# The gates' activations, the log-forget and the decays of an mLSTM block, three pieces of products later

## The chip, the cores and the metric

The kernel runs on one core of a Trainium2 chip. The metric is the device time of one execution in microseconds (us). Before the change the median of three runs is 1558.58 us (1557.95 to 1559.88).

## The reference

Two transformer blocks for 512 tokens of width 1024, in float32. The change touches the mLSTM mixer of the first block. There `proj = h @ w_in + b_in` gives, beside much else, q, k, v and two gates (input gate and forget gate) for each of four heads:

```python
log_f = jax.nn.log_sigmoid(f_pre)
b = jnp.cumsum(lfc, axis=-1)
d_log = jnp.where(causal, b[..., :, None] - b[..., None, :] + ic[..., None, :], -jnp.inf)
m_t = jnp.maximum(inter_log, jnp.max(d_log, axis=-1))
dmat = jnp.exp(d_log - m_t[..., None])
sc = jnp.einsum("bhtd,bhsd->bhts", qc, kc) * dmat
num = (jnp.einsum("bhts,bhse->bhte", sc, vc)
       + inter_w[..., None] * jnp.einsum("bhtd,bhde->bhte", qc, c_st))
```

q and k go through a causal convolution of four taps and a silu first. Another branch puts `a` through a depthwise convolution of 31 taps over 1024 channels.

## The kernel before, in words

Activations lie transposed in SBUF, 128 channels by 512 tokens for each tile. To keep float32's accuracy a product is made in three: both the weights and the activations are split into a high half (float32r) and the rest. A **product** here is one tile of 128 output channels: 16 matmuls with the high half of the activations (`hl`, L1814 with the high half of the weights, `sph`, and L1815 with the low half, `spl`) and 8 with their low half (`lo`, L1822), all into one PSUM bank. `gemm` calls `between()` after each of the two groups of eight of `hl` and after the evacuation; what lies between two such calls is a **piece**, three to a product.

The halves of the weights are made as they are needed. SyncE loads a raw tile (one of four buffers), ScalarE copies it to `sph` (L2032), VectorE subtracts that from the raw tile into `spl` (L2376), which `hl` waits for. Three buffers hold the halves, so the split of a tile can begin when the product two ahead of its own starts. It is placed into the program after the first group of `hl`.

`plan()` writes one list of steps, and each engine runs those that concern it in that order, with semaphores between engines. So an engine that waits holds up all that stands behind it. Four things set where a step comes:

- `later_ops` holds pairs of a number of the count `tick` and a step. `between()` issues those that are due and then counts on.
- `side` is a list of generators. `between()` lets the first of them go on by one `yield`; the next gets its turn when that one has ended.
- `spare` holds the depthwise taps (L2430 on VectorE), given out at a rate of so many for each piece. In these stages the rate is 0 for head 0's first three products and 1 for the fourth and for head 1.
- `heads(h)` for h of 2 or more calls `step()` without a product until the scores of head h - 2 are placed.

The stage in question: after the value products (`gemm_tok`, L1882 to L1884) comes the tile of the gates, w_if (L1861). `gates()` has ScalarE copy its lower half (L2065), VectorE add it (`gates_sum`, L2453), and ScalarE run six activations on 4 rows of 512 with two table loads (`gates`, L2071 to L2080). The generator `decays` then places VectorE's log-forget (`log_forget`, L2459), a memset of POOL that waits for it (L3039), four decays of four dependent instructions each (L2468 to L2476), m's store and reload by POOL's queue, four groups of row copies (L2483, L2486, L2491), five idle yields, and the transposes of these rows on TensorE (L1941, L1943).

Beside it run the products of q and k, four to a head. Each is evacuated by ScalarE (L2088 into `xpad`, L2091 for the first tap into a temporary), gets three more taps on VectorE (L2501, three instructions) and a silu on ScalarE (L2096). `attend(h)` stands behind `decays` in `side`: for each of four key blocks the scores on TensorE (L1949, L1950), their weights `exp` on ScalarE (L2103), and the weighing on VectorE (L2516), and then the value products on TensorE (L1957).

Of the kernel before, what the change touches and what calls it, by code (L numbers as in the profile page):

```python
# [129 lines left out]
def plan():  # L130
# [3 lines left out]
    def add(name, *args):  # L134
        steps.append((name, args))
# [15 lines left out]
    def fence(name):  # L151
        add("fence", name)
# [66 lines left out]
    side, tail, spare, later_ops = [], [], [], []  # L219
    rate, due, tick = [0, 0], [0.0], [0]  # L220
# [306 lines left out]
    for i in range(8):  # L527
# [4 lines left out]
        j, free = tmp.take()  # L532
# [84 lines left out]
    def gates(b, g):  # L617
        j, free = tmp.take()
        k, free2 = tmp.take()
        add("gates_low", b, g, k, free2)  # L620
        add("gates_sum", b, j, free, k)
        later_ops.append((tick[0] + 1, lambda: add("gates", j, k)))
        forget.extend((j, k))
        return [("gate", "sum")]

    forget = []
    gemm_halves("w_if", "n1", gates)
    misc.free += [main.take() for _ in range(LENT)]
    cb, gd, mus = keepc(40), keepc(16), keepc(8)

    def decays():
        yield
        yield
        add("log_forget", *forget)
        for j in forget:
            tmp.give(j, ("lf",))
        k1, free = tmp.take()
        fence("decay")
        add("decay_begin", k1, free, mus)
        for t in range(T):  # L640
            add("decay", t, k1, mus)
            yield
        tmp.give(k1, ("decay", 3))
        add("m_out")
        for k in range(T):
            add("decay_rows", k)
            yield
        for _ in range(5):
            yield
        b, free = misc.take()  # L650
        add("decay_cols", b, free, cb, gd)
        misc.give(b, ("cb",), ("gd",))

    side.append(decays())


# [2554 lines left out]
```

## Time and profile before

| | |
|---|---|
| median of three runs | 1558.58 us |
| lowest, highest | 1557.95, 1559.88 us |
| span of the profiled execution | 1558.7 us |
| instructions | 19501 |
| TensorE (PE) busy | 1535.3 us, 98% |
| VectorE (DVE) busy | 1064.5 us, 68% |
| ScalarE (ACT) busy | 715.5 us, 46% |
| GpSimd (POOL) busy | 133.7 us, 9% |
| chain that ended last | PE 89%, DVE 7%, ACT 2%, issue 1%, DMA 1% |

The span is that of one execution, taken by the profiler; no separate time of that execution is listed, and it lies within the three runs. PE is TensorE, DVE VectorE, ACT ScalarE, POOL GpSimd. Times in rows are us from the span's start. "Idle before" is what an engine stood still ahead of an instruction, with the operation that ended it. L12 is line 12 of the kernel. A buffer's number is left out in the profile.

### The profile page before, as it was taken

Reading aid. Unit: us, or ns where it says so; the run is one execution under the profiler, and the core shown is the slowest. Engines: PE = TensorE matmul, PEld = TensorE weight load, DVE = VectorE, ACT = ScalarE, POOL = GpSimd, SP = SyncE. Lnnn points to the kernel's source line nnn. Section 1 sums busy time; section 2 is a strip of 40 time slices with the busy share of each in tenths; the row PEclk is TensorE's granted clock in tenths of the full one; section 3 lists DMA queues with packets and bytes.
Section 4 is the critical chain, followed back from the end, with each engine's and each line's share of the span. In section 5 each row is a group of like instructions: output and inputs, shape, how many; then the busy total and the mean of one; then the engine's idle time right before and its main releaser. Section 6 shows DMA issues by size and latency. Waiting matters only on the chain.

```text
span 1558.7 us, 19501 instructions
## 1 busy us (share of the span) xinstructions
PE 1535.3 (98%) x7464; PEld 1270.6 (82%) x7464; DVE 1064.5 (68%) x1657; ACT 715.5 (46%) x1069; POOL 133.7 (9%) x131
## 2 busy tenths in 40 slices
PE   8999899999999999999999999999999999999998
PEld 3788677877888899998888787878888888888877
DVE  8998898898888799995753456766476444432356
ACT  5543578764543656653333325446354322222233
POOL 0111000000000111110021011100201101000000
PEclk9999999999999999999999999999999999999999
DMA  9778222233666546657333323111332222323331
GB/s 367 183 187 206 69 94 61 75 95 93 210 238 203 163 127 158 157 148 253 98 110 101 108 85 109 55 41 41 115 132 99 95 95 95 108 86 101 98 135 68
DMA packets 59709, 197.18 MB, mean 127 GB/s; under 512 B 7005, under 2 KB 9309, under 8 KB 59234
## 3 DMA queue, kind: packets, MB, share of 16 engines
q1 hardware_dynamic: 52208, 175.49, 34.3%
q0 software_dynamic: 7408, 20.46, 6.6%
q8 instruction: 59, 0.97, 0.3%
q14 instruction: 32, 0.26, 0.1%
q10 hardware_dynamic: 2, 0.00, 0.0%
HBM read 171.80 MB, written 6.30 MB: 114 GB/s over the span
## 4 chain that ended last, share of the span: by engine, by line
PE 89%; DVE 7%; ACT 2%; issue 1%; DMA 1%; ACTq 0%; POOL 0%; DVEq 0%; POOLq 0%
PE bank L1822 22%; PE bank L1814 22%; PE bank L1815 22%; PE bank L1852 3%; PE bank L1844 3%; PE bank L1843 3%; DVE convout L2430 2%; PE bank L1870 2%; DVE tmp L2501 1%; PE bank L1882 1%; PE bank L1884 1%; PE bank L1883 1%; PE bank L1957 1%; PE bank L1974 1%; DVE spl L2376 1%
## 5 line engine op out<-in xcount | busy, mean ns | idle before, releaser
L1814 PE MATMUL bank<-HH,sph 128*128 128x512 f32 x1192 | 475.7, 399 | 6.9 <-DVE spl L2376 4.7
L1815 PE MATMUL bank<-HH,spl 128*128 128x512 f32 x1192 | 466.0, 391 | 0.0
L2376 DVE TENSOR_TENSOR spl<-raw,sph 128x1024 fp32r<-128x1024 f32 (+1 forms) x206 | 259.8, 1263 | 225.0 <-ACT sph L2032 224.9
L2032 ACT ACTIVATE sph<-raw 128x1024 fp32r<-128x1024 f32 (+1 forms) x227 | 233.0, 1029 | 176.6 <-PE bank L1822 139.5
L1822 PE MATMUL bank<-HL,sph 128*128 128x512 f32 x1192 | 309.7, 394 | 0.0
L1814 PEld LDWEIGHTS bank<-HH,sph 128*128 128x128 f32 x1192 | 225.0, 189 | 58.9 <-issue 10.2
L1815 PEld LDWEIGHTS bank<-HH,spl 128*128 128x128 f32 x1192 | 224.9, 189 | 47.8 <-issue 1.5
L1822 PEld LDWEIGHTS bank<-HL,sph 128*128 128x128 f32 x1192 | 222.7, 188 | 48.6 <-issue 2.4
L2430 DVE SCALAR_TENSOR_TENSOR convout<-convin,vecs,convout 128x512 f32<-128x512 f32 x240 | 165.3, 748 | 0.0
L1814 PE MATMUL bank<-midh,sph 128*128 128x512 f32 x352 | 136.9, 389 | 0.0
L1815 PE MATMUL bank<-midh,spl 128*128 128x512 f32 x352 | 136.9, 389 | 0.0
L1822 PE MATMUL bank<-midl,sph 128*128 128x512 f32 x352 | 87.6, 389 | 0.0
L1815 PEld LDWEIGHTS bank<-midh,spl 128*128 128x128 f32 x352 | 66.1, 188 | 13.7
L1822 PEld LDWEIGHTS bank<-midl,sph 128*128 128x128 f32 x352 | 66.1, 188 | 13.7
L1814 PEld LDWEIGHTS bank<-midh,sph 128*128 128x128 f32 x352 | 66.0, 188 | 13.7
L2243 ACT ACTIVATE midh<-tmp 128x512 fp32r<-128x512 f32 x29 | 18.3, 632 | 109.2 <-DVE tmp L2723 88.0
L3012 POOL TENSOR_TENSOR tmp<-tmp,tmp 128x512 f32<-128x512 f32 x27 | 35.2, 1314 | 315.4 <-ACT tmp L2047 315.4
L1843 PE MATMUL bank<-th,sph 128*128 128x256 f32 x240 | 60.2, 283 | 0.0
L1844 PE MATMUL bank<-th,spl 128*128 128x256 f32 x240 | 60.2, 283 | 0.0
L3061 POOL TENSOR_TENSOR midl<-tmp,midh 128x512 fp32r<-128x512 f32 x22 | 28.5, 1296 | 230.4 <-ACT midh L2243 230.4
L2501 DVE SCALAR_TENSOR_TENSOR tmp<-xpad,vecs,tmp 128x512 f32<-128x512 f32 x48 | 36.0, 751 | 16.6 <-ACT tmp L2091 15.4
L1843 PEld LDWEIGHTS bank<-th,sph 128*128 128x128 f32 x240 | 46.1, 192 | 0.0
(362 smaller groups left out, 2281.0 us busy)
## 6 DMA issues: line engine op xcount, KB each, us to landing
raw<-in_w_in SPq DMA_DIRECT2D x69, 512.0 KB, 3.6
raw<-in_w_up SPq DMA_DIRECT2D x66, 512.0 KB, 3.5
more<-in_w_ada SPq DMA_DIRECT2D x32, 512.0 KB, 5.0
raw<-in_w_down SPq DMA_DIRECT2D x32, 512.0 KB, 3.5
raw<-in_w_gate SPq DMA_DIRECT2D x22, 512.0 KB, 3.2
spl<-raw POOLq DMA_DIRECT2D x18, 512.0 KB, 6.0
ada<-in_w_ada SPq DMA_DIRECT2D x16, 512.0 KB, 10.9
raw<-in_w_down SPq DMA_DIRECT2D x16, 384.0 KB, 3.1
```

The lines of the kernel that those rows point to most:

```text
L1814: e.matmul(P_[b][:], sph(n)[:, q], hi[:, k, :], start=k == 0, stop=False)
L1815: e.matmul(P_[b][:], spl(n)[:, q], hi[:, k, :], start=False, stop=False)
L1822: m = e.matmul(P_[b][:], sph(n)[:, q], low[:, k, :], start=False, stop=last and k == kb - 1)
L1843: e.matmul(to, high_of(which, s)[:, q], x, start=k == 0, stop=False)
L1844: e.matmul(to, low_of(which, s)[:, q], x, start=False, stop=False)
L1852: m = e.matmul(to, high_of(which, s)[:, q], x, start=False, stop=k == 3)
L1870: m = e.matmul(P_[b][:], raw(n)[:, token(k)], FULL[acts][:, k, :], start=k == 0, stop=k == 7)
L2032: e.activation(sph(n), raw(n), ACT.Copy).then_inc(*up("s_w_high", ("wh", n)))
L2376: e.tensor_tensor(spl(n), raw(n), sph(n).bitcast(F32), ALU.subtract).then_inc(*up("s_w_low", ("wl", n)))
L2430: ins = e.scalar_tensor_tensor(CO[:, i, :], src, wt, CO[:, i, :], ALU.mult, ALU.add)
L2501: e.scalar_tensor_tensor(TMP[j][:], XP[:, s, k:k + 512], wt, TMP[j][:], ALU.mult, ALU.add).then_inc(*up("s_qk_conv", ("qk_conv", h, z, k)))
L3012: e.tensor_tensor(TMP[a][:], TMP[a][:], TMP[j][:], ALU.add).then_inc(*up("s_sum_p", ("ss", name, i)))
```

## The change

The gates' six activations come due three counts of `tick` later, and `decays` yields five times instead of twice before its first step. Line 622 and lines 632 to 633 change, nothing else.

```diff
@@ -619,7 +619,7 @@
         k, free2 = tmp.take()
         add("gates_low", b, g, k, free2)
         add("gates_sum", b, j, free, k)
-        later_ops.append((tick[0] + 1, lambda: add("gates", j, k)))
+        later_ops.append((tick[0] + 4, lambda: add("gates", j, k)))
         forget.extend((j, k))
         return [("gate", "sum")]
 
@@ -629,8 +629,8 @@
     cb, gd, mus = keepc(40), keepc(16), keepc(8)
 
     def decays():
-        yield
-        yield
+        for _ in range(5):
+            yield
         add("log_forget", *forget)
         for j in forget:
             tmp.give(j, ("lf",))
```

The order of ScalarE's instructions behind the high half of product 3's weights (`sph_60<-raw_57`), product 1 being the first of head 0. `sph_58<-raw_54` is the high half of product 4's weights. Before:

```order
L2032 ACTIVATE sph_60<-raw_57 128x1024
L2071 ACTIVATE row_137<-tmp_86,vecs 4x512
L2073 ACTIVATE tmp_86<-tmp_86,vecs 4x512
L2076 ACTIVATE tmp_88<-tmp_86 4x512
L2078 ACT_TABLE_LOAD
L2078 ACTIVATE tmp_88<-tmp_88 4x512
L2080 ACT_TABLE_LOAD
L2080 ACTIVATE tmp_88<-tmp_88 4x512
L2088 ACTIVATE xpad<-bank,vecs 128x512
L2091 ACTIVATE tmp_91<-xpad,vecs 128x512
L2032 ACTIVATE sph_58<-raw_54 128x1024
L2096 ACT_TABLE_LOAD
```

And with the change:

```order
L2032 ACTIVATE sph_60<-raw_57 128x1024
L2088 ACTIVATE xpad<-bank,vecs 128x512
L2091 ACTIVATE tmp_91<-xpad,vecs 128x512
L2032 ACTIVATE sph_58<-raw_54 128x1024
L2071 ACTIVATE row_137<-tmp_86,vecs 4x512
L2073 ACTIVATE tmp_86<-tmp_86,vecs 4x512
L2076 ACTIVATE tmp_88<-tmp_86 4x512
L2078 ACT_TABLE_LOAD
L2078 ACTIVATE tmp_88<-tmp_88 4x512
L2080 ACT_TABLE_LOAD
L2080 ACTIVATE tmp_88<-tmp_88 4x512
L2096 ACT_TABLE_LOAD
```

The evacuation of product 1 and the high half for product 4 now stand ahead of the gates' chain, and the chain ahead of product 1's silu and product 2's evacuation.

VectorE at the same place, from the low half of product 3's weights (`spl_63`) on; `spl_61<-raw_54` is product 4's and `spl_62<-raw_55` product 5's. Before:

```order
L2376 TENSOR_TENSOR spl_63<-raw_57,sph_60 128x1024
L2501 SCALAR_TENSOR_TENSOR tmp_91<-xpad,vecs,tmp_91 128x512 x3
L2459 SCALAR_TENSOR_TENSOR row_138<-tmp_86,tmp_88 4x512
L2468 SCALAR_TENSOR_TENSOR row_139<-tmp_89,row_138 4x128
L2471 TENSOR_TENSOR row_140<-row_137,row_139 4x128
L2473 SCALAR_TENSOR_TENSOR mrow<-row_140,kept 4x128
L2476 TENSOR_TENSOR kept<-mrow,row_139 4x1
L2376 TENSOR_TENSOR spl_61<-raw_54,sph_58 128x1024
```

With the change:

```order
L2376 TENSOR_TENSOR spl_63<-raw_57,sph_60 128x1024
L2501 SCALAR_TENSOR_TENSOR tmp_91<-xpad,vecs,tmp_91 128x512 x3
L2376 TENSOR_TENSOR spl_61<-raw_54,sph_58 128x1024
L2501 SCALAR_TENSOR_TENSOR tmp_89<-xpad,vecs,tmp_89 128x512 x3
L2459 SCALAR_TENSOR_TENSOR row_138<-tmp_86,tmp_88 4x512
L2468 SCALAR_TENSOR_TENSOR row_139<-tmp_87,row_138 4x128
L2471 TENSOR_TENSOR row_140<-row_137,row_139 4x128
L2473 SCALAR_TENSOR_TENSOR mrow<-row_140,kept 4x128
L2476 TENSOR_TENSOR kept<-mrow,row_139 4x1
L2376 TENSOR_TENSOR spl_62<-raw_55,sph_59 128x1024
```

The log-forget and the first decay have moved from ahead of product 4's low half to ahead of product 5's. The other three decays and the row copies move one product on in the same way.

VectorE around the first weighing of head 0 (`sc<-bank`, 128x512); the three taps L2501 next to it are those of product 7 before, and of product 8 with the change. Before:

```order
L2501 SCALAR_TENSOR_TENSOR tmp_86<-xpad,vecs,tmp_86 128x512 x3
L2430 SCALAR_TENSOR_TENSOR convout<-convin,vecs,convout 128x512
L2376 TENSOR_TENSOR spl_63<-raw_55,sph_60 128x1024
L2430 SCALAR_TENSOR_TENSOR convout<-convin,vecs,convout 128x512 x2
L2501 SCALAR_TENSOR_TENSOR tmp_91<-xpad,vecs,tmp_91 128x512 x3
L2516 SCALAR_TENSOR_TENSOR sc<-bank,tmp_88 128x512
L2430 SCALAR_TENSOR_TENSOR convout<-convin,vecs,convout 128x512
L2376 TENSOR_TENSOR spl_61<-raw_56,sph_58 128x1024
L2516 SCALAR_TENSOR_TENSOR sc<-bank,tmp_86 128x384
```

With the change:

```order
L2501 SCALAR_TENSOR_TENSOR tmp_86<-xpad,vecs,tmp_86 128x512 x3
L2430 SCALAR_TENSOR_TENSOR convout<-convin,vecs,convout 128x512
L2376 TENSOR_TENSOR spl_61<-raw_56,sph_58 128x1024
L2430 SCALAR_TENSOR_TENSOR convout<-convin,vecs,convout 128x512 x2
L2501 SCALAR_TENSOR_TENSOR tmp_89<-xpad,vecs,tmp_89 128x512 x3
L2516 SCALAR_TENSOR_TENSOR sc<-bank,tmp_88 128x512
L2430 SCALAR_TENSOR_TENSOR convout<-convin,vecs,convout 128x512
L2516 SCALAR_TENSOR_TENSOR sc<-bank,tmp_86 128x384
L2516 SCALAR_TENSOR_TENSOR sc<-bank,tmp_88 128x256
```

The first weighing stands behind one more low half (`spl_61<-raw_56`, product 10's) and one more triple of taps, and the four weighings stand close together. On TensorE the scores move one product on, and the last two of head 0 are placed by `heads(2)` without products between them; the first value product L1957 stands ahead of product 9 in both.

## Rows read from the trace of the kernel before

**Rows 1.** Page, busy us (share of the span) x instructions
```profile
PE 1535.3 (98%) x7464; PEld 1270.6 (82%) x7464; DVE 1064.5 (68%) x1657; ACT 715.5 (46%) x1069; POOL 133.7 (9%) x131
```
**Rows 2.** Waits, TensorE, whole run: us in total, times, longest
```profile
PE bank L1814 <- DVE spl L2376: 4.7, 1, 4.7
...
PE bank L1957 <- DVE sc L2516: 1.2, 1, 1.2
...
PE bank L1968 <- DVE tmp L2441: 0.9, 1, 0.9
```
**Rows 3.** Timeline, TensorE: start, us, engine, line, [idle before <- releaser]
```profile
172.72 1.97 PE L1822 MATMUL bank<-HL,sph 128*128 128x512 f32 x8
179.44 0.77 PE L1814 MATMUL bank<-HH,sph 128*128 128x512 f32 x1 [4.74 <-DVE spl L2376]
...
183.73 0.40 PE L1814 MATMUL bank<-HH,sph 128*128 128x512 f32 x1
...
186.92 0.47 PE L1814 MATMUL bank<-HH,sph 128*128 128x512 f32 x1
...
215.93 0.67 PE L1957 MATMUL bank<-vtok,sc 128*128 128x257 f32 x2 [1.16 <-DVE sc L2516]
```
**Rows 4.** Timeline, ScalarE, 165 to 176
```profile
165.66 0.72 ACT L2071 ACTIVATE row<-tmp,vecs 4x512 f32<-4x512 f32 x1 [5.70 <-DVE tmp L2453]
...
171.71 0.69 ACT L2088 ACTIVATE xpad<-bank,vecs 128x512 f32<-128x512 f32 x1
...
173.15 1.04 ACT L2032 ACTIVATE sph<-raw 128x1024 fp32r<-128x1024 f32 x1
...
175.64 0.63 ACT L2096 ACTIVATE qk<-tmp 128x512 f32<-128x512 f32 x1
```
**Rows 5.** Timeline, VectorE, 160 to 187
```profile
160.98 4.06 DVE L2430 SCALAR_TENSOR_TENSOR convout<-convin,vecs,convout 128x512 f32<-128x512 f32 x6
...
173.28 2.33 DVE L2501 SCALAR_TENSOR_TENSOR tmp<-xpad,vecs,tmp 128x512 f32<-128x512 f32 x3 [4.53 <-ACT tmp L2091]
175.64 0.68 DVE L2459 SCALAR_TENSOR_TENSOR row<-tmp,tmp 4x512 f32<-4x512 f32 x1
...
178.09 1.21 DVE L2376 TENSOR_TENSOR spl<-raw,sph 128x1024 fp32r<-128x1024 f32 x1
...
184.23 0.41 DVE L2468 TENSOR_TENSOR_SCAN row<-tmp,row 4x128 f32<-4x128 f32 x1
...
185.57 1.21 DVE L2376 TENSOR_TENSOR spl<-raw,sph 128x1024 fp32r<-128x1024 f32 x1
```
**Rows 6.** Groups by line, VectorE, 165 to 216: busy us, mean ns | idle before
```profile
L2486 DVE TENSOR_SCALAR rowc<-rowc,row 4x128 f32<-4x128 f32 x6 | 1.6, 274 | 0.2
...
L2483 DVE COPY rowc<-row 4x128 f32<-4x128 f32 x4 | 0.8, 208 | 0.0
...
L2491 DVE TENSOR_TENSOR row<-mrow,row 4x512 f32<-4x512 f32 x1 | 0.7, 671 | 0.0
```
**Rows 7.** Timeline, ScalarE, 208 to 212: table load, weights of head 0
```profile
208.82 1.28 ACT L2103 ACT_TABLE_LOAD   x1
210.11 1.28 ACT L2103 ACTIVATE tmp<-tmp,kept 128x128 f32<-128x128 f32 x4
211.30 0.67 ACT L2088 ACTIVATE xpad<-bank,vecs 128x512 f32<-128x512 f32 x1
```
**Rows 8.** Windows: us, busy PE, PEld, DVE, ACT, POOL, granted clock, DMA share, GB/s
```profile
179.40:183.80 4.40, 4.36 (x11) 3.48 (x12) 4.09 (x11) 0.00 (x0) 0.00 (x0) 0.52 0.37 119
...
215.00:240.00 25.00, 24.07 (x101) 19.09 (x102) 20.81 (x44) 19.00 (x29) 0.54 (x1) 1.00 0.24 74
```
**Rows 9.** Timeline, VectorE, 212 to 239
```profile
212.85 2.33 DVE L2501 SCALAR_TENSOR_TENSOR tmp<-xpad,vecs,tmp 128x512 f32<-128x512 f32 x3 [1.60 <-ACT tmp L2091]
215.10 0.68 DVE L2516 SCALAR_TENSOR_TENSOR sc<-bank,tmp 128x512 f32<-128x512 f32 x1
...
238.36 2.33 DVE L2501 SCALAR_TENSOR_TENSOR tmp<-xpad,vecs,tmp 128x512 f32<-128x512 f32 x3 [2.90 <-ACT tmp L2091]
```

## The prediction

> **What bounds the kernel now.** I read the busy times first: TensorE is busy for 98% of the span and VectorE for 68% [rows 1]. So time is saved or lost only where TensorE stands still or runs slowly. Next the waits of TensorE over the whole run [rows 2]: the longest by far is 4.7 us for VectorE's L2376, the low half of a weight tile. One more of the three shown lies near the change, 1.2 us of L1957 for VectorE's L2516.
>
> I number the products behind w_if: 1 to 4 are head 0, 5 to 8 head 1, from 9 on head 2. In TensorE's timeline [rows 3] the long wait is in front of product 4: free at 174.70, started at 179.44, product 5 at 186.92. The short one is in front of L1957, the first value product of head 0, at 215.93. ScalarE's timeline [rows 4] shows why product 4 is late. The gates' chain starts at 165.66, when VectorE has made the sum of line 2453, and holds ScalarE until 171.71: 6.05 us, two table loads in it. Behind it stand the evacuation of product 1 (L2088, L2091), done on TensorE since 163.8, and the high half of product 4's weights, at 173.15. VectorE then does three taps of the query convolution, the log-forget and the first decay before L2376 at 178.09 [rows 5].
>
> **What the change moves.** Nothing is added, and by the order of instructions two table loads of ScalarE go. SP and POOL issue the same things in the same order: the memset at L3039, the store of m and its broadcast load only come one product later, and the first reader of that load (L2506) stands over 10 us behind it in both orders. From product 9 on all engines have the same order as before, but for the numbers of temporaries. So I walk the three engines from 163.8 to the first value product, with durations as distances between starts, so that overlaps of neighbours are taken off.
>
> VectorE [rows 5]: a depthwise tap 0.66 (six in 4.06, less one overlap of 0.08); three query taps 2.24 (2.33 less the overlap); a low half 1.14 (1.22 less the overlap); a decay of four instructions 1.36 (184.23 to 185.57); log-forget with its wait for POOL's memset 1.11 (175.64 to 178.09 holds both it and a decay). The ten decay rows and the sum of line 2491 together 3.0, overlaps taken off [rows 6]. ScalarE [rows 4]: L2088 and L2091 1.44 (171.71 to 173.15; the result 0.1 later), a high half 1.06, a silu 0.54; a table load with four weights 2.48 (208.82 to 211.30 [rows 7]), 1.28 of it the load. A product of 24 matmuls is 5.44 at full clock, 0.227 each (eight of L1822 take 1.97, with 0.39 for the last [rows 3]).
>
> Step 1, product 4. Product 3 ends at 174.70, so products 1 and 2 ended at 163.8 and 169.3, 5.44 apart. ScalarE evacuates product 1 from 163.86, makes the high half at 165.30 and starts the gates' chain at 166.36. VectorE does the taps of product 1 at 168.68 and the low half at 170.92. It is there at 172.1; TensorE wants it at 174.54 (172.72 plus eight of 0.227 [rows 3]). The wait of 4.74 goes.
>
> Step 2, what is late next. The gates' chain now stands ahead of the evacuation of product 2: chain to 172.41, table load to 173.69, silu 0.54, L2088 and L2091 at 174.23 and 174.95, taps of product 2 on VectorE at 175.80 (it had been idle 3.7, where before it was idle 4.5 ahead of the taps of product 1). From there VectorE does not stop: taps 2.24, log-forget 1.11, first decay 1.36, low half of product 5 at 180.5. Product 5 starts at 181.9: a wait of 1.9. Between that low half and the next lie three decays and the taps of product 3: product 6 starts at 189.3, 2.0 late. Then come the decay rows, which one product later meet three depthwise taps, where before they met none: product 7 at 197.0, 2.2 late. So of the 5 us won at product 4, most has been given back here.
>
> Why so little is left: before, product 4 ran at half clock. The profile grants 0.52 from 179.4 to 183.8 [rows 8], that is the 1.2 GHz level, after 4.74 us idle, and product 4 took 7.48 instead of 5.44. But these 2.0 us cost nothing: low half 5 began at 185.57 and was there at 186.8, so that product 5 could not have started before 186.9 in any case. The stretch is bound by VectorE. Its work is not made less by the change.
>
> Step 3, the first value product (L1957). It waits for the first weighing (L2516). Before, what VectorE does ahead of that ends with the taps of product 7. Now the scores come one product later, and the taps of product 8, the low half of product 10 and three depthwise taps stand ahead of it as well: 2.24 + 1.14 + 3 x 0.66 = 5.4 us more work. Walked from 175.80: five triples of taps 11.2, log-forget 1.1, four decays 5.4, five low halves 5.7, decay rows 3.0, eleven depthwise taps 7.3, L2495 and L2506 0.7; sum 34.4. So the taps of product 7 start at 210.2, where before they did at 212.85 after 1.60 idle [rows 9]. They end at 212.55. Then ScalarE does silu, a table load and four weights (to 215.6), L2088 and L2091 of product 8 (result at 217.1), VectorE its taps (to 219.4) and the weighing (0.68). The value product starts at 220.2. TensorE is ready for it at 212.8: a wait of 7.4 in place of 1.16. The value product stood at 215.93, so it comes **4.3 us later**. The same walk through the order before gives 215.7, with all waits of TensorE in it to 0.3 us, so the method holds where I can test it.
>
> Step 4, the clock. TensorE has then been idle for 7.4 us; the nearest row is the 4.74 us, after which the granted clock was 0.5 until some 4 us into the work and ten matmuls took 4.29 instead of 2.27 [rows 3, 8]: 2.0 us. Here nothing hides it. VectorE and ScalarE have caught up at the value product, and further on VectorE idles (2.9 us ahead of 238.36 [rows 9]) and waits for what follows TensorE. From below the price is 0: after the 1.16 us idle at 215.93 the clock stayed at 1.00 [rows 8]. From above I take 4.1: half clock for twice as long as that row. I take **2.0**, as 7.4 us is past the 4.74 and nothing shown is nearer. The same fall at products 5 to 7 would cost nothing, since 1.7 us more there ends within the next wait.
>
> The Trainium skill (TensorE: Matmul & The Clock Gate, Part 1) says that the default state is throttled, that activity releases it, and that the point at which it does varies from run to run. By that rule the 2.0 would be somewhat more or less in each run; the sum does not use it.
>
> The two table loads saved are 2.6 us of ScalarE between the weights of head 0, where it waits for L2516 now; on the path nothing. A load takes 1.28, and the next activation starts 0.01 behind it (208.82 to 210.11 [rows 7]). The Trainium skill (ScalarE: Activation LUTs, What ACT_TABLE_LOAD costs) adds a drain of about 1.38 us to each switch, which would set the taps of product 2 back by 4.1 us and give about 1569. The rows show no such drain, and the sum goes by them.
>
> Sum: 4.3 + 2.0 = 6.3 us, on the profiled execution's span of 1558.7 gives 1565.0. The median of the runs is 1558.6, 0.1 below that span, so nothing has to be shifted. Behind 216 TensorE waits for VectorE once more for 0.9 (L1968 [rows 2]). It moves along with TensorE's work; at most 0.9 is absorbed there, which I leave to the range.
>
> **Rivals.**
> *The clock stays, or its fall is not exposed.* Then only step 3 counts: 1558.7 + 4.3 = 1563.0. Against it: 4.74 us idle were enough. For it: in the trace there is one such fall after a single wait, and its timing against the work is chance. 0.20.
> *The lead is kept (faster).* The long wait goes with its slow matmuls, 4.74 + 2.04 = 6.8, and VectorE has enough idle time to absorb the decays: 1552. It decides at the low halves of products 5 to 7: each must be there 5.44 us after the one before. By rows 5 VectorE needs 7.3 to 7.6 between them, so this is unlikely. 0.04.
> *Moved, not changed.* The waits in front of products 5 to 7 take the place of the one in front of product 4, but the value product is not later than before, as it would be if the query taps and the weighing did not queue as I read: 1558.7, give or take 2. 0.09.
> *Worse than forecast.* The taps that are pushed together also delay the weighing of the later parts, or the half clock costs up to its bound: 1558.7 + 4.3 + 4.1 = 1567.1. 0.07.
> *Switches of ScalarE cost more than their loads.* Three of them stand on the path ahead of the taps of product 2. The gap behind a load is 0.01 in rows 7; with 0.5 us at each the result would be 1566.5. Nothing in the trace speaks for it. The Trainium skill's drain (the page named above) is this rival at its largest. 0.02.
> The forecast itself: 0.58.
>
> **How the numbers follow.** A measurement of this kernel can tell about 0.2%, 3.1 us, from no change. Slower by more than that is above 1561.7: forecast, clock rival and worse one, 0.87. Within: 0.09. Faster: 0.04. The range goes from 1561.5 (the clock rival with the 0.9 absorbed and some spread of runs) to 1567.5 (the worse one); the last two rivals on the other side are left out.
>
> **What would show it.** In the changed kernel's waits: no wait ahead of product 4; three waits of L1814 for L2376 of about 2 us each, at 180, 187 and 195; one wait of L1957 for L2516 of about 7 us, ending near 220; and behind it matmuls 0.43 apart for some 4 us, with a granted clock of 0.5. VectorE should show no idle time between 176 and 215 but for a few tenths. I am wrong if L1957's wait is under 3 us or VectorE has gaps in that stretch; if the wait is there but the matmuls behind it are at full clock, only step 4 fails.

## The result, and the profile after

| | before | changed |
|---|---|---|
| median | 1558.58 us | 1564.99 us |
| lowest to highest, 5 runs each | 1557.95 to 1559.88 | 1563.55 to 1565.85 |
| span of the profiled execution | 1558.7 us | 1561.4 us |
| own time of that execution | not listed | 1563.55 us |
| TensorE, VectorE, ScalarE busy | 1535.3, 1064.5, 715.5 us | 1535.8, 1064.4, 713.3 us |

The ratio is 1.0037, with a 95% interval of 1.0026 to 1.0048: 6.4 us slower, where the 0.2% bound is 3.1.

The page's busy times and, from the table of TensorE's waits (us in total, times, longest), the three rows that answer to [rows 2]:

```profile
PE 1535.8 (98%) x7464; PEld 1271.6 (81%) x7464; DVE 1064.4 (68%) x1657; ACT 713.3 (46%) x1067; POOL 133.9 (9%) x131
...
PE bank L1814 <- DVE spl L2376: 5.4, 3, 1.9
...
PE bank L1957 <- DVE sc L2516: 3.7, 1, 3.7
...
PE bank L1968 <- DVE tmp L2441: 0.8, 1, 0.8
```

One wait of 4.7 has become three with 5.4 in all, the wait of the first value product has grown from 1.2 to 3.7, and that of L1968 is what it was. TensorE's timeline (start, busy us, line, [idle before <- releaser]), against [rows 3]:

```profile
154.88 1.98 PE L1861 MATMUL bank<-HL,sph 128*128 128x512 f32 x8
...
180.30 0.47 PE L1814 MATMUL bank<-HH,sph 128*128 128x512 f32 x1 [1.68 <-DVE spl L2376]
...
187.78 0.47 PE L1814 MATMUL bank<-HH,sph 128*128 128x512 f32 x1 [1.79 <-DVE spl L2376]
...
195.39 0.47 PE L1814 MATMUL bank<-HH,sph 128*128 128x512 f32 x1 [1.93 <-DVE spl L2376]
...
218.76 0.67 PE L1957 MATMUL bank<-vtok,sc 128*128 128x257 f32 x2 [3.65 <-DVE sc L2516]
...
221.01 0.63 PE L1814 MATMUL bank<-HH,sph 128*128 128x512 f32 x1
221.44 0.63 PE L1815 MATMUL bank<-HH,spl 128*128 128x512 f32 x1
```

First a correction that every comparison below needs. The opening of the kernel differs from execution to execution by one or two us. The last eight matmuls of w_if, ahead of everything that the change moves, start at 154.88 here and in the profile of before, in the same view, at 156.40:

```profile
156.40 1.98 PE L1861 MATMUL bank<-HL,sph 128*128 128x512 f32 x8
```

So 1.52 us are added to the times of after. I call a time *aligned* when it has been shifted so that this row stands at 156.40. Aligned, products 5, 6 and 7 start at 181.82, 189.30 and 196.91, and the first value product at 220.28, 4.35 later than before.

ScalarE's timeline, against [rows 4]: the gates' chain (five activations with two table loads, L2071 to L2080; the description above counts six) now stands behind the evacuation of product 1 and ahead of that of product 2.

```profile
164.73 0.70 ACT L2071 ACTIVATE row<-tmp,vecs 4x512 f32<-4x512 f32 x1
...
170.75 1.28 ACT L2096 ACT_TABLE_LOAD   x1
172.04 0.63 ACT L2096 ACTIVATE qk<-tmp 128x512 f32<-128x512 f32 x1
...
173.29 0.82 ACT L2091 ACTIVATE tmp<-xpad,vecs 128x512 f32<-128x512 f32 x1
```

VectorE's timeline, against [rows 5] and [rows 9]:

```profile
174.14 2.32 DVE L2501 SCALAR_TENSOR_TENSOR tmp<-xpad,vecs,tmp 128x512 f32<-128x512 f32 x3 [3.54 <-ACT tmp L2091]
176.49 0.68 DVE L2459 SCALAR_TENSOR_TENSOR row<-tmp,tmp 4x512 f32<-4x512 f32 x1
...
178.94 1.21 DVE L2376 TENSOR_TENSOR spl<-raw,sph 128x1024 fp32r<-128x1024 f32 x1
...
186.42 1.21 DVE L2376 TENSOR_TENSOR spl<-raw,sph 128x1024 fp32r<-128x1024 f32 x1
...
208.65 2.32 DVE L2501 SCALAR_TENSOR_TENSOR tmp<-xpad,vecs,tmp 128x512 f32<-128x512 f32 x3
...
215.68 2.33 DVE L2501 SCALAR_TENSOR_TENSOR tmp<-xpad,vecs,tmp 128x512 f32<-128x512 f32 x3 [1.59 <-ACT tmp L2091]
217.93 0.68 DVE L2516 SCALAR_TENSOR_TENSOR sc<-bank,tmp 128x512 f32<-128x512 f32 x1
```

Between 174.14 and the 1.59 us ahead of 215.68 it doesn't stand idle, but for 0.43 us ahead of the first decay, as before. The last row is the first weighing, which the first value product waits for. Two low halves, 7.5 us apart (178.94 and 186.42), are what TensorE waits for ahead of products 5 and 6. Last the granted clock, in windows of after (us, busy PE, PEld, DVE, ACT, POOL, clock, DMA share, GB/s):

```profile
196.30:203.20 6.90, 6.90 (x28) 5.27 (x27) 6.83 (x10) 2.97 (x4) 0.00 (x0) 0.51 0.31 94
203.20:215.00 11.80, 11.80 (x50) 8.77 (x48) 10.75 (x16) 9.66 (x15) 0.00 (x0) 1.00 0.32 99
218.70:220.00 1.30, 1.24 (x6) 1.09 (x7) 1.30 (x3) 0.87 (x3) 0.00 (x0) 1.00 0.00 0
220.20:223.70 3.50, 3.50 (x10) 2.76 (x9) 2.57 (x4) 3.10 (x4) 0.54 (x1) 0.51 0.32 81
```

The clock is at its lower level (1.2 GHz) twice: in product 7, behind the three waits, and from 1.4 us behind the start of the value product.

**Where the 6.4 us are.** Aligned, L1968 starts at 381.54 (380.02 as shown), before at 375.58: 5.96 later, which is the 4.35 of the value product and 1.6 of the half clock from 220.2 to 223.7. The difference is the same 5.9 at 1023, and the 0.4 that is left lies well within the interval (4.1 to 7.5 us). The two *spans* differ by only 2.7 us, and that must not be read as the size of the change: 1.52 is the opening, and the profile of before lost 1.7 us at 1026.7, where this window of before shows a fall that the profile of after doesn't have:

```profile
1026.70:1030.10 3.40, 3.40 (x8) 2.20 (x7) 3.03 (x8) 1.65 (x5) 0.00 (x0) 0.50 0.32 101
```

4.35 + 1.6 - 1.7 - 1.5 = 2.75.

### The profile page after: what moved, and what is told of

It reads as the page before. It is cut to its first block, busy times and chain, and to the rows that moved or that the text cites. A ratio compares the mean times of both kernels' runs of the same rounds, so it can differ in the third digit from the quotient of the medians.

```text
span 1561.4 us, 19499 instructions
## 1 busy us (share of the span) xinstructions
PE 1535.8 (98%) x7464; PEld 1271.6 (81%) x7464; DVE 1064.4 (68%) x1657; ACT 713.3 (46%) x1067; POOL 133.9 (9%) x131
## 4 chain that ended last, share of the span: by engine, by line
PE 90%; DVE 7%; ACT 2%; issue 1%; ACTq 0%; DVEq 0%; POOL 0%; POOLq 0%
PE bank L1822 22%; PE bank L1814 22%; PE bank L1815 22%; PE bank L1852 3%; PE bank L1844 3%; PE bank L1843 3%; PE bank L1870 2%; PE bank L1882 1%; PE bank L1884 1%; PE bank L1883 1%; DVE convout L2430 1%; DVE tmp L2501 1%; PE bank L1957 1%; PE bank L1974 1%; DVE spl L2376 1%
## 5 line engine op out<-in xcount | busy, mean ns | idle before, releaser
L2501 DVE SCALAR_TENSOR_TENSOR tmp<-xpad,vecs,tmp 128x512 f32<-128x512 f32 x48 | 36.0, 750 | 21.5 <-ACT tmp L2091 20.3
```

The lines of the kernel that those rows point to most:

```text
L2501: e.scalar_tensor_tensor(TMP[j][:], XP[:, s, k:k + 512], wt, TMP[j][:], ALU.mult, ALU.add).then_inc(*up("s_qk_conv", ("qk_conv", h, z, k)))
```

## The experiments

Theory A is that of the prediction: VectorE's queue sets when the products behind w_if and the first value product can start, a walk through the three engines' queues gives the times, and a fall of the clock costs only where nothing waits behind it. The rivals, B and C where they have letters, put the loss on something else: on the lateness of the log-forget as such, or on TensorE's own lateness and clock in that stretch. Times of before in the three sets of runs: medians 1559.14 (18 runs), 1559.29 (30) and 1559.40 (18). Each set has its own runs of before beside it, and the ratios are taken against those. Where a diff is against the changed kernel, it says so.

### The gates alone

```
-        later_ops.append((tick[0] + 1, lambda: add("gates", j, k)))
+        later_ops.append((tick[0] + 4, lambda: add("gates", j, k)))
```

> Half of the change: the gates' activations three counts later, decays as before. Theory A (VectorE's queue sets the pace; the walk over the three engines): the wait ahead of product 4 shrinks to 1.7 us, since the log-forget still stands ahead of its low half and waits for the chain; product 5 waits 2.0 us more; the first value product comes 3.1 us earlier than before. Time near 1555.5 us, slower by up to 2 if a fall of the clock is exposed. Theory B (the decays and the gates cost the same wherever they stand, and the change lost its time to the clock alone): within 1 us of before. Theory C (the wait ahead of product 4 with its slow matmuls is the whole cost): it goes or nearly goes, 1552 to 1553.

1555.86 us (1554.41 to 1557.51), ratio 0.9978, interval 0.9969 to 0.9987: faster. TensorE's timeline (the aligned times are 0.50 earlier):

```profile
176.59 0.47 PE L1814 MATMUL bank<-HH,sph 128*128 128x512 f32 x1 [1.40 <-DVE spl L2376]
...
184.07 0.47 PE L1814 MATMUL bank<-HH,sph 128*128 128x512 f32 x1 [1.76 <-DVE spl L2376]
...
213.07 0.67 PE L1957 MATMUL bank<-vtok,sc 128*128 128x257 f32 x2 [1.16 <-DVE sc L2516]
```

The value product stands at 212.57 aligned, 3.4 *earlier* than before, where 3.1 was expected. Half of the change is a gain. The gain over before is 2.0 to 4.8 us by the interval, so theory B (within 1 us) falls, and C's 1552 to 1553 lies below every run.

### The decays alone

```
     def decays():
-        yield
-        yield
+        for _ in range(5):
+            yield
```

> The other half: gates as before, the decays' generator three yields later. Theory A: product 4 waits 2.3 us, 5 1.5, 6 2.0, 7 2.2, the first value product 7.5; it starts 6.4 us later than before, and with 2.0 us for the half clock behind it the time is near 1567. Theory B: no better or worse than the change but for the clock, 1560 to 1565. Theory C: as the wait ahead of product 4 goes down by more than half, faster than before by 2 to 4 us.

1568.65 us (1567.57 to 1568.73), ratio 1.0058 (1.0045 to 1.0072). The waits, and the clock behind the last of them:

```profile
PE bank L1814 <- DVE spl L2376: 7.1, 4, 2.2
PE bank L1957 <- DVE sc L2516: 6.7, 1, 6.7
```

```profile
220.70:227.60 6.90, 5.51 (x13) 4.43 (x14) 5.54 (x9) 4.23 (x7) 0.54 (x1) 0.51 0.18 52
```

The value product is at 222.34 aligned, 6.4 late as expected. At L1968 the delay is 8.9 us (384.26 as shown by the profile, 384.51 aligned), so the half clock from the start at 222.09 to 227.6 costs 2.5 more. The medians give 9.5, 1.6 more than theory A's 1567; B and C, both faster than this, fall. The two parts add up: -3.3 and +9.5 give +6.2 by the medians, the whole change +6.4; by the starts of L1968, -3.4 and +8.9 give +5.5 against +6.0.

### The whole change, with the transposes and scores where they were

Against the changed kernel:

```
             add("decay_rows", k)
             yield
-        for _ in range(5):
+        for _ in range(2):
             yield
```

> The whole change, but with two idle yields instead of five ahead of the transposes of the decays' rows, so that the scores of head 0 stand where they did before. Theory A: the transposes now wait 6 us for the last row of the decays in the middle of product 6; the first value product comes 1.8 us later than before instead of 4.4. With a half clock behind the 6 us wait, 2 us, near 1562.4; without it 1560.4. Theory B: as the change, 1564 to 1566.

1564.23 us (1561.62 to 1564.41), ratio 1.0029 (1.0019 to 1.0039), over what theory A gave and inside theory B's 1564 to 1566. By the time alone this run speaks for B. The timeline (aligned 0.51 earlier) and a window:

```profile
198.16 1.20 PE L1941 MATMUL bank<-consts,rowc 4*128 4x4 f32 x10 [6.26 <-DVE row L2491]
...
221.34 0.59 PE L1957 MATMUL bank<-vtok,sc 128*128 128x257 f32 x2
```

```profile
194.90:205.20 10.30, 7.04 (x27) 5.89 (x28) 10.19 (x18) 5.06 (x7) 0.00 (x0) 0.50 0.23 64
```

The trace tells it otherwise. The wait has only moved, from L1957 to the decays' transposes, 6.26 us where 6 were expected. Behind it TensorE worked at 0.50 for 7.04 us, which is 3.5 us lost, and its own work reached the value product last, without a wait: at 220.83 aligned, 4.9 later than before and not 1.8. The runs fall into two groups, five at 1564.2 to 1564.4 and three at 1561.6 to 1562.2; my 1562.4 fits the second, and the first has the lower mean clock (0.995 to 0.997 against 0.998). So this run doesn't separate A from B as it was meant to.

### The whole change, with taps taken out of the stretch

Against the changed kernel, twelve of the fifteen depthwise taps of heads 0 and 1 (three to each product of rate 1) are put off to heads 2 and 3:

```
-TAPS = [[0, 0, 0, 1], [1, 1, 1, 1], [1, 1, 1, 1], [1, 1, 1, 1], [1.6, 1.6, 1.6, 1.6], [1.6, 1.6, 1.6, 1.6],
+TAPS = [[0, 0, 0, 0], [0, 0, 0, 1], [1.5, 1.5, 1.5, 1.5], [1.5, 1.5, 1.5, 1.5], [1.6, 1.6, 1.6, 1.6], [1.6, 1.6, 1.6, 1.6],
```

> The whole change, with the twelve depthwise taps of products 4 to 8 but for three given out during heads 2 and 3 instead (rates 0, then 1.5 for each piece). Order on TensorE and ScalarE is that of the change. Theory A: with seven fewer taps ahead of the first weighing VectorE gets there 4.4 us earlier, the value product starts within 0.2 us of where it did before, after a wait of about 5 us at full clock for all; 1558.7 if no fall of the clock is exposed, 1560.6 if one is, plus what the taps cost in their new place (0 to 2 us). Theory B: as the change, 1564 to 1566, since TensorE's and ScalarE's orders are the same.

1563.66 us (1563.21 to 1564.97), ratio 1.0031 (1.0019 to 1.0044): a miss, and close to theory B's 1564, though the wait of product 7 is gone. Three rows of TensorE's timeline and one of ScalarE's:

```profile
216.72 0.94 PE L1957 MATMUL bank<-vtok,sc 128*128 128x257 f32 x2 [4.60 <-DVE sc L2516]
...
315.37 0.47 PE L1814 MATMUL bank<-HH,sph 128*128 128x512 f32 x1 [1.33 <-DVE spl L2376]
...
320.26 1.10 PE L1949 MATMUL bank<-qk 128*128 128x512 f32 x2 [1.00 <-ACT qk L2096]
```

```profile
198.57 0.63 ACT L2096 ACTIVATE qk<-tmp 128x512 f32<-128x512 f32 x1 [3.27 <-PE bank L1943]
```

Aligned, the value product is at 217.66: 2.6 earlier than in the changed kernel, but 1.7 later than before, where I had expected 0.2. In VectorE's timeline 2 taps stand ahead of the first weighing in place of 14, not seven fewer as I had counted, so some 7.9 us of its work are gone; in their place it stands idle ahead of the taps of products 6, 7 and 8 (2.72, 1.78 and 2.25 us, against 1.59 ahead of product 8 alone). Less work for VectorE does bring the value product forward, but only until the other engines set the pace. I read two of their delays as the cause: the silu of product 5, which waits for TensorE's transposes (L1943), and a half clock before it (0.55 in the window 189.3 to 193.0). No run takes them away one by one. In their new place the taps cost 2.0 us: the wait of 1.33, and 0.66 more at L1949 than the 0.34 there in the profile of after.

### The change and the kernel before, with TensorE kept busy in its waits

Matmuls whose result nobody reads are put ahead of four places of the changed kernel, and ahead of one of the kernel before:

```
+FILL = {(1, 0): 2, (1, 1): 2, (1, 2): 2, "vals": 8}
...
+    def fill(n):
+        b, free = main.take()
+        add("warm", b, free, (512,) * n, False)
+        main.give(b)
...
+            if (h, z) in FILL:
+                fill(FILL[h, z])
             gemm("w_in", 16 + i, 8, "n1", qk_tile(h, z, i, toks, used))
```

For the kernel before it is `FILL = {(0, 3): 5}`.

> The whole change, with matmuls that nobody reads (128x512, fp32, 0.86 us each) put ahead of products 5, 6 and 7 (two each) and ahead of the first value product (eight), so that TensorE isn't idle where it waits. They go into banks that are given back at once, and VectorE's and ScalarE's queues are the same as with the change. Theory A (VectorE's queue sets the first value product at 220.2, +4.3; the rest of the loss is a clock that falls behind the waits): the first value product still starts at 220.3 (shift of the opening taken out), the granted clock is 1.00 from 176 to 235, and the time is about 1.7 us under the change's 1565.0: 1563.3 (1562.8 to 1564.0). Theory C (TensorE's own lateness or speed in this stretch counts, not VectorE's queue): the value product comes earlier by what the half clock at product 7 costs, some 3 us, and the time is under 1562. If the clock costs nothing, the time stays at 1565.

> The kernel before with five such matmuls ahead of product 4, in its wait of 4.74 us, so that product 4 runs at full clock. Theory A (the low half of product 5 waits for VectorE at 185.6 either way): product 4 ends up to 2 us earlier, product 5 stays where it was (186.8), and the time is that of before within 0.3 us. Theory C (the half clock at product 4 cost the kernel before its 2.0 us): 1557.1, that is 2 us less than the 1559.1 of before in the last runs.

The changed kernel filled: 1564.02 us (1562.32 to 1565.99), ratio 1.0028 (1.0017 to 1.0038). The value product (it is L1968 there, since the added lines move the numbers by 11) and the window:

```profile
222.85 0.67 PE L1968 MATMUL bank<-vtok,sc 128*128 128x257 f32 x2
```

```profile
176.00:235.00 59.00, 58.79 (x239) 42.19 (x238) 47.77 (x83) 33.89 (x52) 1.73 (x4) 1.00 0.25 80
```

This execution's opening was 2.55 us longer, so aligned the value product is at 220.30: unchanged to 0.02 us, though product 7 had lost 3.4 us to the half clock before. That start alone proves little, since the eight fillers ahead of it begin at 215.98 and, at 0.86 us each, end just then. The first weighing on VectorE doesn't stand behind them, and it is the row to compare:

```profile
222.01 0.68 DVE L2527 SCALAR_TENSOR_TENSOR sc<-bank,tmp 128x512 f32<-128x512 f32 x1
```

Aligned it starts at 219.46, in the changed kernel at 219.45. So the loss in product 7 was free, and theory C falls. The four-matmul operation that answers to L1968 of the change starts at 379.86 aligned, 1.7 us earlier than there: this is what the exposed half clock had cost. The medians differ by 1.0 us, and against the before of its own set each is 6.4 and 4.7 us slower, but the intervals overlap; by the times alone the 1.7 isn't shown. The median of 1564.02 lies at the upper end of what was expected.

The kernel before filled: 1558.98 us (1558.56 to 1560.96) against 1559.29, ratio 1.0003 (0.9994 to 1.0011). Lines are 9 higher, aligned times 0.34 later:

```profile
179.10 0.47 PE L1823 MATMUL bank<-HH,sph 128*128 128x512 f32 x1 [0.45 <-DVE spl L2385]
...
186.58 0.47 PE L1823 MATMUL bank<-HH,sph 128*128 128x512 f32 x1 [1.79 <-DVE spl L2385]
...
215.59 0.67 PE L1966 MATMUL bank<-vtok,sc 128*128 128x257 f32 x2 [1.17 <-DVE sc L2525]
```

Aligned these are 179.44, 186.92 and 215.93, the very numbers of [rows 3]. Product 4 ran at full clock, and what it won became a wait of 1.79 ahead of product 5. That holds for more than the profiled execution: the mean clock is 0.998 to 1.000 in the eleven runs, with six at 1.000, against 0.996 to 0.998 in the thirty of before, and the time is the same.

### Gates three later, log-forget one later

```
-        later_ops.append((tick[0] + 1, lambda: add("gates", j, k)))
+        later_ops.append((tick[0] + 4, lambda: add("gates", j, k)))
...
-        yield
-        yield
+        for _ in range(3):
+            yield
         add("log_forget", *forget)
...
-        for _ in range(5):
+        for _ in range(3):
             yield
```

> Gates three pieces later as in the change, but the log-forget and the decays one piece later, not three, and three empty pieces behind the decay rows, not five. All taps as before. Theory A, by the same walk through the queues of the three engines that gave the six value products so far within 0.3 us (with the clock's falls put in): the wait of product 4 stays gone, product 5 waits 1.2, the transposes of the decays 2.8, the first value product starts at 211.3 (before 215.9, gates alone 212.6), and product 10 is done 4.4 us ahead of before: 1554.7 (1553.5 to 1556.5, the upper end for a half clock of up to 2 us). Theory B (any delay of the log-forget loses what it delays): slower than the gates alone by 1 to 2 us, 1557.

1557.13 us (1554.96 to 1559.58), ratio 0.9990 (0.9981 to 0.9998): above my range, no better than the gates alone, and theory B's 1557. The trace shows two delays that B doesn't speak of. The timelines of VectorE, GpSimd and TensorE:

```profile
173.89 0.41 DVE L2468 TENSOR_TENSOR_SCAN row<-tmp,row 4x128 f32<-4x128 f32 x1 [1.56 <-POOL kept L3039]
```

```profile
173.67 0.09 POOL L3039 MEMSET kept<- 4x1 f32 x1 [32.43 <-ACT qk L2096]
```

```profile
181.60 0.47 PE L1814 MATMUL bank<-HH,sph 128*128 128x512 f32 x1 [2.10 <-DVE spl L2376]
...
190.08 0.75 PE L1941 MATMUL bank<-consts,rowc 4*128 4x4 f32 x10 [2.77 <-DVE row L2491]
```

The first decay stood 1.56 us behind a 0.09 us memset of GpSimd. `fence("decay")` is recorded right behind the log-forget, so with one more yield the silu of product 1 is already in ScalarE's queue ahead of it, and the memset waits for that. The expectation had 0.43 for this wait, as before. The 211.3 expected for the value product, 1.7 for the clock's fall behind the wait of 2.77 (191.0 to 194.6 at 0.53) and 1.1 for the longer wait give 214.1; measured 214.16. This sum was made afterwards; the kernel with the fence ahead tests its last term.

### The same with fewer taps

Against the last kernel: four empty yields in place of three, and

```
-TAPS = [[0, 0, 0, 1], [1, 1, 1, 1], [1, 1, 1, 1],
+TAPS = [[0, 0, 0, 0], [0, 0, 1, 1], [1.5, 1.5, 1.5, 1.5],
...
```

> As the last one with four empty pieces, and three fewer taps of the convolution handed to VectorE during heads 0 and 1 (they go to head 2, at 1.5 a piece). Theory A: product 5 waits 1.2, product 6 1.1, the first value product starts at 209.7, product 10 is done 6.1 us ahead of before; the moved taps give back 0 to 1.5 us in head 2, since four taps moved so cost 2.3 in an earlier run: 1553.8 (1552.5 to 1555.5). Rival: the taps cost all of it back, 1555 or over, no better than the one without them.

1557.16 us (1555.23 to 1560.57), ratio 0.9987 (0.9979 to 0.9996): the rival's result. The value product was at 211.38 aligned, earlier than in any run so far, and it was given back at the end of the stage:

```profile
374.26 2.08 PE L1968 MATMUL bank<-tmp,ones 128*128 128x512 f32 x2 [2.15 <-DVE tmp L2441]
```

Nine taps were taken out (three products of three pieces each; where the expectation says three taps and four, the kernels move nine and twelve) and, at 1.5 for the twelve pieces of head 2, six put back. I read the longer wait (0.85 before) as the three taps that were left over; the last kernel below takes up all nine. The wait is 1.3 of the 2.8 us that the value product was ahead of the last kernel. A fall of the clock behind it, 0.51 in the window 374.2 to 377.7, is 1.7 us more, and together they take all of it. The profiled execution is the slowest of the eleven (1560.57).

### The fence ahead, TensorE filled, and the taps again

Three kernels. The first is the one with gates three and log-forget one later, with one line moved:

```
     def decays():
+        fence("decay")
         for _ in range(3):
             yield
...
-        fence("decay")
```

The second adds one filler ahead of product 5 and two ahead of the decays' transposes:

```
+FILL = {(1, 0): 1, 'dc': 2}
...
+        fill(FILL["dc"])
         b, free = misc.take()
         add("decay_cols", b, free, cb, gd)
```
 The third has the fence ahead, four empty yields, the fewer taps with 1.75 in place of 1.5, and one filler each ahead of products 5 and 6.

> The kernel with gates +3 and log-forget +1, with one line moved: the fence that GpSimd's memset of the running maximum waits for is recorded ahead of the empty pieces, not behind the log-forget. Theory A with the wait that the walk had missed (VectorE's first scan stood 1.56 us behind that memset, which stood behind ScalarE's silu of product 1, since the fence was recorded after that silu had been queued): the wait is 0.4 or less, the low half of product 5 and all behind it on VectorE come 0.8 us earlier (product 5 starts at 181.3 with the opening's shift taken out, not 182.2), and the time is 0.8 us under that of 1557.1: 1556.3 (1554.5 to 1557.3, since the clock's falls differ from run to run). If the memset is not what VectorE waits for (it is only the last semaphore of several), nothing moves: 1557.1.

> The last one with matmuls that nobody reads (128x512, 0.86 us each) in its two waits of TensorE: one ahead of product 5, two ahead of the transposes of the decays. Theory A: no clock fall behind those waits (granted clock 1.00 from 176 to 235), first value product at 211.3 to 211.6, time 1 to 2 us under the last one's where that one falls: 1554.9 (1554.0 to 1556.3). Rival: the fillers cost what they save, since the waits are shorter than they are (the first is 1.2 by the walk): no gain over the last one.

> Three fewer taps in heads 0 and 1 and three more in head 2 (at 1.75 a piece; at 1.5 one was left over for the end of the stage, where the wait of L1968 grew from 0.8 to 2.2), four empty pieces, the fence early, and one filler ahead of products 5 and 6 each. Theory A: first value product at 209.7 (the run with 1.5 a piece had 211.4, of which 0.8 was the fence and 0.6 the clock), the wait of L1968 back at 0.8, and the time 5.5 us under before: 1553.6 (1552.5 to 1555.5). Rival: the taps in head 2 give back all of it through a later wait: 1555.5 or over.

The fence ahead: 1556.95 us (1556.26 to 1558.43), ratio 0.9982 (0.9974 to 0.9991). VectorE's and TensorE's timelines:

```profile
173.16 0.41 DVE L2468 TENSOR_TENSOR_SCAN row<-tmp,row 4x128 f32<-4x128 f32 x1
```

```profile
180.87 0.47 PE L1814 MATMUL bank<-HH,sph 128*128 128x512 f32 x1 [0.58 <-DVE spl L2376]
```

The wait for the memset is gone entirely, not only down to 0.4, so product 5 starts 1.5 us earlier (180.72 aligned) and the value product too (212.61 against 214.16). The medians show 0.2 of that, where the runs of the kernel it is compared with lie up to 4.6 us apart: in the trace a gain, in the times not shown. The value product now stands where the gates alone had it (212.57), so with the fence early, putting the log-forget off by one piece costs nothing there, but it wins nothing either.

Filled: 1555.82 us (1553.98 to 1557.60), ratio 0.9976 (0.9965 to 0.9986). The granted clock is 1.00 from 176 to 235, and the value product starts at 211.03 aligned, 1.6 earlier. The median is 1.1 us lower, with intervals that overlap.

With the taps: 1554.05 us (1552.87 to 1556.13), ratio 0.9964 (0.9952 to 0.9977), 5.4 us under before and the best here. TensorE's timeline (lines 9 higher, aligned 1.35 earlier):

```profile
281.50 0.50 PE L1823 MATMUL bank<-HH,sph 128*128 128x512 f32 x1 [0.88 <-ACT tmp L2136]
...
371.43 1.12 PE L1977 MATMUL bank<-tmp,ones 128*128 128x512 f32 x2 [0.84 <-DVE tmp L2450]
```

The end of the stage is back at its 0.84, as it should be if the left-over taps had caused the 2.15 (the fence and the fillers changed as well). The value product is at 209.39, 1.6 earlier than without the taps' move; a new wait of 0.88 at 281.5 takes part of it, and the stage ends only 0.5 us earlier. Between these two kernels the intervals overlap.

## Why the prediction was right

**What bounds the stretch** (VectorE, and its work is not made less): right. The filled kernel before shows it directly, with three starts reproduced to 0.01 us.

**Step 1**, the wait of product 4 goes: right; no wait is listed there.

**Step 2**, products 5, 6 and 7: forecast 181.9, 189.3 and 197.0, aligned 181.82, 189.30 and 196.91; waits 1.68, 1.79 and 1.93, forecast 1.9, 2.0 and 2.2. The rival that keeps the lead fell with this, and the one in which the value product stays where it was fell with step 3.

**Step 3**, the value product 4.3 later: measured 4.35. The taps of product 7 were forecast for 210.2 and start at 210.17 aligned, those of product 8 for 217.1 and start at 217.20. The *wait* was forecast at 7.4 and is 3.65, with the same end: product 7 ran at half clock (196.3 to 203.2 at 0.51), which made TensorE reach the value product 3.4 us later. The text had said that such a fall would cost nothing there, and the unmoved weighing of the filled changed kernel shows that it didn't. But the number that it gave to be looked for was the one without the fall, and its bound for being wrong (under 3 us) was nearly met for a reason that had nothing to do with the theory. A start is a better thing to forecast than a wait.

**Step 4**, the clock: forecast 2.0, measured 1.6 to 1.7 (between the value product and L1968; and against the filled kernel). Right in mechanism, slightly too large, and the size is in part luck. My reason was the 7.4 us of idle time; the clock fell after 3.65. In the decays alone, where the wait was 6.67 us, the fall cost 2.5. The text also says that the trace of before has one such fall behind a single wait. It has a second, at 1026.7 behind a wait of 1.42 us (the window above), which would have told that waits far below 4.74 us can be enough.

The Trainium skill (TensorE: Matmul & The Clock Gate, Part 1) says that the point at which activity releases the clock varies from run to run. No run here measures that point, but the falls vary as well: behind the same wait of 1.42 us at the transposes near 1024, the clock fell in the profile of before (1026.7 to 1030.1 at 0.50) and not in that of after.

**ScalarE's table loads**: no drain shows. Behind the load at 170.75, 1.28 long, the silu starts at 172.04, 0.01 later. The Trainium skill (ScalarE: Activation LUTs, What ACT_TABLE_LOAD costs) would have added some 1.38 us to each; the measured row decides against it.

**The sum** was set on a span of 1558.7 as if a time lay 0.1 under its span. That was not so. Wherever a span and its own time are both listed, the time is 2.1 to 2.2 above it (here 1563.55 and 1561.4). The profiled execution of before, taken above for one that lies within the three runs, would then be a run of 1560.9, longer than the median by the 1.7 of its fall at 1026.7 and some more. Both offsets were left out, and they cancel: a step that was right in its number only. The forecast as a difference, 6.3, stands on its own against 6.4. In the chances, the three terms named for "slower" add to 0.85; the 0.87 holds with the 0.02 of the switches.

**The wait of L1968**: 0.84 as before, nothing absorbed.

**What I had not seen** is that the change is two changes with opposite signs. The gates three pieces later are worth 3.3 us; the log-forget and decays three pieces later cost 9.5. Put through each part alone for the first two experiments, the walk gave the sign of both and the shift of the value product to 0.3 us.

## What to carry to other kernels

Put each part of a reordering through the walk alone: here one line of the change made the kernel faster and another took that back almost three times over (3.3 and 9.5 us). Time won in front of an engine that another one feeds is only won if the feeder can keep the new pace, and an added yield also moves what a fence records: a 0.09 us memset on an otherwise idle engine held the critical queue for 1.56 us. Align two profiles on the last row ahead of the change before comparing any start, and don't compare spans.

## What the runs showed of the hardware

- A span and its own time differ by nearly the same here, 2.1 to 2.2 us, in every run that lists both.
- The granted clock falls to its lower level behind waits of 1.4 to 2.8 us as well (1.42 in the profile of before near 1024, 1.93 behind two like it in that of after, 2.77 with gates three and log-forget one later), and not always behind the same one. With fillers in the waits it stayed at 1.00 from 176 to 235 in the profiles of all four filled kernels. The gates alone, without fillers and with waits of 1.40 and 1.76, show no fall there either, so one profile is no proof for the fillers.
- Half clock costs nothing while another engine is late by more: 3.4 us in product 7 of the change and 2.0 in product 4 of before were free; 1.6 to 1.7 behind the value product were not, nor most of the 3.5 behind the transposes with the scores kept.
- Of a fall behind a wait the first matmuls may still run at full clock (218.7 to 220.0 at 1.00, then 0.51).
